# Four 512-column products, then four 256-column ones: the order of TensorE's products in a hybrid mLSTM / RG-LRU / ConvFFN block

## The chip, the cores and the metric

The kernel runs on one core of one Trainium2 chip. The metric is the device time of one execution in microseconds (us). Three runs of the kernel before took 1136.75, 1137.09 and 1137.92 us; the median is 1137.09 us. What this measurement tells from no change is about 0.2% of it, some 2.3 us.

## What is computed

One layer of a streaming encoder over 256 rows of 2048 numbers, all float32:

```python
n1 = rmsnorm(x, norm_mix_g)
q, k, v, o_pre, if_pre, x_r, g_r = split(n1 @ w_in)          # 2048 x (4*1024 + 8 + 2*1024)
h_m = sigmoid(o_pre) * mlstm_chunkwise(q, k, v, i_pre, f_pre)  # 4 heads of 256
h_r = rglru(x_r, ...) * gelu(g_r)                             # 8 blocks of 128
x = x + concat(h_m, h_r) @ w_out                              # 2048 x 2048
gate, up = split(rmsnorm(x, norm_ffn_g) @ w_up)               # 2048 x 2 * 5632
x = x + (silu(causal_dwconv(gate)) * up) @ w_down             # 5632 x 2048
y = rmsnorm(x, norm_final_g)
```

## The kernel before

Nearly all the time is four matrix products with weights that are read once from HBM, 512 KB at a time. TensorE gets them in the type fp32r, and the precision of float32 is kept by splitting each operand in two: a high part (the value rounded to fp32r, written by ScalarE, called ACT in the profile) and a low part (the value minus its high part, written by VectorE, DVE). A product is then high x high + high x low + low x high.

**Projections** (w_in and w_up). The 2048 numbers of a row are 16 k-tiles of 128. `xT[:, kt, 0, :]` holds the high part of k-tile kt of the transposed, normalised input (128 partitions x 256 rows of x), `xT[:, kt, 1, :]` the low part. A **group** is 256 output columns over all 16 k-tiles. Its weights come in four **units** s = 0 to 3 of CH = 4 k-tiles each, in the four slots of a ring: `raw[:, s]` as loaded, `w[:, s, c, 0, :]` the high and `w[:, s, c, 1, :]` the low part of k-tile c of the unit. A group adds up in two banks of PSUM, `ps[:, 2 * pair + n, :]` with n = 0 and 1 for its two halves of 128 outputs; `pair` alternates between groups. In one bank, columns 0 to 255 gather high x high, and columns 256 to 511 the two mixed products. So each k-tile and each n has one product of 512 columns ("full": 128 columns of high weights stand in the array, and the high and low parts of xT stream past) and one of 256 columns ("rest": the low weights stand, the high part of xT streams). For the group of v (`rows_out=True`) the two operands change roles, with the same sizes. Every product has stationary data of its own, 128 x 128, so every product has one load (LDWEIGHTS).

`part_of_unit` writes these products, for a range of k-tiles; `unit` waits until the low weights of a slot are there (`lo_ready`), calls it for four k-tiles and lets the last product signal `unit_used`, which lets ACT write that slot's next weights; `group` waits for the group's banks (`group_free`) and runs four units. There are 24 groups with w_in (q, k of head 0; then v, o, x_r and g_r of each head, and q, k of the next), and 44 with w_up: 68 groups of 64 products, 4352 products in all. In the first group, `after(pe, tiles, ...)` also waits for the low part of each two k-tiles of xT.

**Contractions** (w_out and w_down, function `contraction`, line L1190): here every product is 512 columns wide, and n, the inner loop, alternates between two banks. They aren't touched.

Between groups of a head TensorE also does plain float32 products: scores (L1133, L1135), the weighted values (L1143 to L1146), a row sum (L1151), the RG-LRU gates (L1161). The order on every engine is the order of the code; nothing is scheduled. The lines that the change touches are L1066 (512 columns) and L1068 (256 columns), and for v L1062 and L1064:

Of the kernel before, what the change touches and what calls it, by code (L numbers as in the profile page):

```python
# [33 lines left out]
P = 128  # L34
D = 2048
S = 256
KT = D // P
# [14 lines left out]
CH = 4  # L52
COLS = 256
# [58 lines left out]
def hybrid_block(nc, x, w_in, w_out, w_up, w_down, wa, wx, gate_w, par_in, const_in, gfin_in, out):  # L112
    with ExitStack() as ctx:
# [3 lines left out]
        def sb(name, shape, dt=F32, where=ctx):  # L117
            return where.enter_context(nc.sbuf_tensor(name, shape, dt))
# [4 lines left out]
        xT = sb("xT", [P, KT, 2, S], F32R)  # L123
        raw = sb("raw", [P, RING, HALF])
        w = sb("w", [P, RING, CH, 2, COLS], F32R)
# [64 lines left out]
        ps = ctx.enter_context(nc.psum_tensor("ps", [P, 8, BANK], F32))  # L190
# [56 lines left out]
        def after(eng, steps, name, i=0):  # L247

            eng.wait_ge(steps.sem, steps.after(name, i))
# [783 lines left out]
        def _(pe):  # L1033
            mm = nc.tensor.matmul
# [16 lines left out]

            def part_of_unit(s, pair, tiles_of_k, rows_out=False, tiles=None):

                for c in tiles_of_k:
                    kt = s * CH + c
                    if tiles and c % 2 == 0:
                        after(pe, tiles, f"t{kt // 2}")
                    for n in range(2):
                        full, rest = ps[:, 2 * pair + n, :], ps[:, 2 * pair + n, COLS:2 * COLS]
                        cut = slice(n * P, (n + 1) * P)  # L1060
                        if rows_out:
                            mm(full, xT[:, kt, 0, cut], w[:, s, c, :, :].rearrange("p a n -> p (a n)"),  # L1062
                               start=kt == 0, stop=False)
                            ins = mm(rest, xT[:, kt, 1, cut], w[:, s, c, 0, :], start=False, stop=kt == KT - 1)  # L1064
                        else:
                            mm(full, w[:, s, c, 0, cut], xT[:, kt, :, :].rearrange("p a n -> p (a n)"),  # L1066
                               start=kt == 0, stop=False)
                            ins = mm(rest, w[:, s, c, 1, cut], xT[:, kt, 0, :], start=False, stop=kt == KT - 1)  # L1068
                return ins

            def unit(g, s, pair, rows_out=False, tiles=None):

                pe.wait_ge(lo_ready, g * RING + (s + 1 + RING))
                part_of_unit(s, pair, range(CH), rows_out, tiles).then_inc(unit_used, 1)
# [8 lines left out]
            for n in range(WARM_UP):  # L1083
                ins = mm(ps[:, B_DEN, 0:P], ones[:], ones[:], start=True, stop=True)  # L1084
# [15 lines left out]
            pe.wait_ge(group_free, 1)  # L1100
            pe.wait_ge(first_lo_ready, 1)
            part_of_unit(0, 0, range(CH // 2), tiles=V0)
            transpose_x(1)
            pe.wait_ge(lo_ready, RING + 1)
            part_of_unit(0, 0, range(CH // 2, CH), tiles=V0).then_inc(unit_used, 1)
            transpose_x(2)
            unit(0, 1, 0, tiles=V0)
# [4 lines left out]
            for kt in range(KT):  # L1112
                ins = mm(ps[:, B_SC, :], gws[:, kt, :, :].rearrange("p a n -> p (a n)"),  # L1113
                         xT[:, kt, :, :].rearrange("p a n -> p (a n)"), start=kt == 0, stop=kt == KT - 1)
# [175 lines left out]
```

## Time and profile before

| | |
|---|---|
| median of three runs | 1137.09 us |
| span of the profiled execution | 1135.8 us |
| TensorE products (PE) | busy 1125.2 us, 99% |
| TensorE loads (PEld) | busy 968.0 us, 85% |
| VectorE (DVE), ScalarE (ACT), GpSimd (POOL) | 749.2, 578.7, 51.6 us |
| HBM | 188 GB/s over the span |

A row of TensorE's products shows its start, which is measured, and an end that is modelled and lies behind the start of the next product, since products are pipelined. How long a product holds the engine is therefore read from start to start. "PEclk" is the granted clock of TensorE in tenths of full speed in the page, and as a share of it in the windows view; full speed is 2.4 GHz.

### The profile page before, as it was taken

The page shows a single profiled execution, that of the slowest core. Times are in us where ns is not written, and L with a number is a line of the kernel's source. Part 1 is how long each engine was busy: PE and PEld are TensorE (multiplying, and loading weights), DVE is VectorE, ACT ScalarE, POOL GpSimd, SP SyncE. Part 2 cuts the span into 40 slices and gives each one's busy share as a digit, 9 for nine tenths or more (in the row PEclk, how much of TensorE's full clock was granted, in tenths as well). Part 3 has the DMA queues.
Part 4 walks back from the last instruction along what each step waited for, and adds up shares of the span by engine and source line. Part 5 has one row for each costly group of instructions (what it writes and reads, how often), then busy time and mean ns, then how long its engine had stood idle before and what let it go on. Part 6 is the DMA issues. An engine that isn't in the chain of part 4 may idle for free.

```text
span 1135.8 us, 18132 instructions
## 1 busy us (share of the span) xinstructions
PE 1125.2 (99%) x6030; PEld 968.0 (85%) x6030; DVE 749.2 (66%) x989; ACT 578.7 (51%) x768; POOL 51.6 (5%) x48
## 2 busy tenths in 40 slices
PE   9999999999999999999999999999999999999997
PEld 8888888888888888888888888888888888888886
DVE  6768576595776686666666666766666655556554
ACT  6656464564665664344434444443544545555454
POOL 0100100100000000000000000000000000002000
PEclk9999999999999999999999999999999999999999
DMA  8756657657555466656665665666566565655653
GB/s 265 226 161 186 191 150 205 167 166 194 183 199 196 153 185 206 190 161 215 191 184 173 211 190 165 204 201 186 167 208 195 190 196 190 194 192 186 196 190 114
DMA packets 166617, 213.56 MB, mean 188 GB/s; under 512 B 6940, under 2 KB 149532, under 8 KB 166464
## 3 DMA queue, kind: packets, MB, share of 16 engines
q1 hardware_dynamic: 165456, 210.40, 60.2%
q0 software_dynamic: 560, 2.24, 0.6%
q10 hardware_dynamic: 576, 0.60, 0.2%
q8 instruction: 15, 0.25, 0.1%
q14 instruction: 10, 0.08, 0.0%
HBM read 211.10 MB, written 2.11 MB: 188 GB/s over the span
## 4 chain that ended last, share of the span: by engine, by line
PE 95%; DVE 3%; ACT 1%; issue 0%; DVEq 0%; ACTq 0%
PE ps L1066 41%; PE ps L1190 27%; PE ps L1068 20%; PE ps L1062 3%; PE ps L1064 1%; DVE w L612 1%; PE ps L1161 0%; PE ps L1041 0%; DVE aT L618 0%; ACT w L351 0%; PE ps L1084 0%; PE ps L1113 0%; PE ps L1143 0%; PE ps L1133 0%; DVE xT L663 0%
## 5 line engine op out<-in xcount | busy, mean ns | idle before, releaser
L1066 PE MATMUL ps<-xT,w 128*128 128x512 f32 x2048 | 716.7, 396 | 1.0 <-DVE w L678 0.5
L612 DVE TENSOR_TENSOR w<-raw,w 128x1024 fp32r<-128x1024 f32 x391 | 479.1, 1237 | 342.9 <-ACT w L351 341.9
L351 ACT ACTIVATE w<-raw 128x1024 fp32r<-128x1024 f32 (+1 forms) x393 | 409.7, 1055 | 417.2 <-PE ps L1068 247.6
L1068 PE MATMUL ps<-xT,w 128*128 128x256 f32 x2048 | 569.2, 278 | 0.0
L1066 PEld LDWEIGHTS ps<-xT,w 128*128 128x128 f32 x2048 | 384.2, 188 | 91.1 <-DVE w L612 1.0
L1068 PEld LDWEIGHTS ps<-xT,w 128*128 128x128 f32 x2048 | 385.2, 188 | 0.2
L1190 PE MATMUL ps<-w,aT 128*128 128x512 f32 x1440 | 327.9, 389 | 0.9 <-DVE aT L618 0.9
L1190 PEld LDWEIGHTS ps<-w,aT 128*128 128x128 f32 x1440 | 269.8, 188 | 57.6 <-DVE aT L618 1.7
L351 ACT ACTIVATE fs<-fc 128x512 f32<-128x512 f32 x22 | 13.9, 632 | 101.0 <-DVE fc L962 101.0
L1025 POOL TENSOR_TENSOR fs<-fs,rB 128x512 f32<-128x512 f32 x22 | 28.4, 1293 | 569.5 <-ACT fs L351 569.5
L1062 PE MATMUL ps<-w,xT 128*128 128x512 f32 x128 | 45.2, 398 | 0.0
L618 DVE TENSOR_TENSOR aT<-act,aT 128x256 fp32r<-128x256 f32 x88 | 38.9, 442 | 0.0
L962 DVE SCALAR_TENSOR_TENSOR fc<-fg,par,fc 128x256 f32<-128x256 f32 x88 | 36.6, 477 | 0.0
L1064 PE MATMUL ps<-w,xT 128*128 128x256 f32 x128 | 35.8, 280 | 0.0
L351 ACT ACTIVATE aT<-act 128x256 fp32r (+1 forms) x88 | 35.3, 401 | 0.0
L351 ACT ACT_TABLE_LOAD x23 | 29.5, 1283 | 2.6 <-issue 2.2
L1062 PEld LDWEIGHTS ps<-w,xT 128*128 128x128 f32 x128 | 24.0, 188 | 5.9
L1064 PEld LDWEIGHTS ps<-w,xT 128*128 128x128 f32 x128 | 24.1, 189 | 0.0
L958 DVE TENSOR_SCALAR fc<-fg,par 128x256 f32<-128x256 f32 x44 | 16.2, 410 | 4.1 <-DVE fg L952 4.0
L969 DVE TENSOR_TENSOR act<-fu,fs 128x512 f32 (+1 forms) x22 | 15.2, 693 | 4.9 <-DVE fu L623 4.8
L351 ACT ACTIVATE xn<-xres 128x512 f32<-128x512 f32 (+3 forms) x15 | 13.3, 889 | 8.6 <-DVE xres L898 8.6
L663 DVE SCALAR_TENSOR_TENSOR xT<-ps,par,xT 128x256 fp32r<-128x256 f32 x32 | 13.3, 477 | 6.2 <-ACT xT L351 6.2
(147 smaller groups left out, 391.8 us busy)
## 6 DMA issues: line engine op xcount, KB each, us to landing
raw<-w_up_dram SPq DMA_DIRECT2D x176, 512.0 KB, 4.6
raw<-w_in_dram SPq DMA_DIRECT2D x95, 512.0 KB, 3.9
raw<-w_down_dram SPq DMA_DIRECT2D x88, 512.0 KB, 4.6
raw<-w_out_dram SPq DMA_DIRECT2D x32, 512.0 KB, 4.6
xres<-x_dram SPq DMA_DIRECT2D x3, 512.0 KB, 7.8
y_dram<-xn SPq DMA_DIRECT2D x3, 384.0 KB, 3.1
bc<-rows POOLq DMA_DIRECT2D x4, 256.0 KB, 6.9
gfin<-gfin_dram POOLq DMA_DIRECT2D x1, 1024.0 KB, 4.6
```

Source lines behind the costliest of these rows:

```text
L351: return sc.activation(out_, in_, fn, **kw)
L612: v.tensor_tensor(w[:, s, :, 1, :], raw[:, s, :].rearrange("p (c n) -> p c n", c=CH), w[:, s, :, 0, :], ALU.subtract).then_inc(lo_ready, 1)
L618: v.tensor_tensor(aT[:, s, 1, :], src[:, bass.ds(first + s, 1), :].rearrange("p a n -> p (a n)"), aT[:, s, 0, :], ALU.subtract).then_inc(a ...
L958: did(v.tensor_scalar(fc[:, b, :], tap, fpar(b, k), fpar(b, FTAPS), ALU.mult, ALU.add), V3, f"c{b}_{k}")
L962: did(v.scalar_tensor_tensor(out=fc[:, b, :], in0=tap, scalar=fpar(b, k), in1=fc[:, b, :], op0=ALU.mult, op1=ALU.add), V3, f"c{b}_{k}")
L969: did(v.tensor_tensor(act[:, bass.ds(j * 2, 2), :], fu[:], fs[:], ALU.mult), V3, "act")
L1025: did(nc.gpsimd.tensor_tensor(fs[:], fs[:], rB[:].to_broadcast([P, 2, S]), ALU.mult), L3, "fs_r")
L1062: mm(full, xT[:, kt, 0, cut], w[:, s, c, :, :].rearrange("p a n -> p (a n)"), start=kt == 0, stop=False)
L1064: ins = mm(rest, xT[:, kt, 1, cut], w[:, s, c, 0, :], start=False, stop=kt == KT - 1)
L1066: mm(full, w[:, s, c, 0, cut], xT[:, kt, :, :].rearrange("p a n -> p (a n)"), start=kt == 0, stop=False)
L1068: ins = mm(rest, w[:, s, c, 1, cut], xT[:, kt, 0, :], start=False, stop=kt == KT - 1)
L1190: ins = mm(ps[:, bank0 + 2 * r + n, :], aT[:, s, a_part, cut], w[:, s, 2 * n:2 * n + 2, w_part, :], start=opens and s == 0 and a_part == 0 ...
```

## The change

The four k-tiles of a unit are taken two by two. For each two, the four 512-column products come first (k-tile c0 with n = 0 and 1, then c0 + 1 with n = 0 and 1), then the four 256-column products in the same order. Before, each 512-column product was followed by the 256-column product of the same k-tile and bank.

```diff
-                for c in tiles_of_k:
-                    kt = s * CH + c
-                    if tiles and c % 2 == 0:
-                        after(pe, tiles, f"t{kt // 2}")
-                    for n in range(2):
-                        full, rest = ps[:, 2 * pair + n, :], ps[:, 2 * pair + n, COLS:2 * COLS]
-                        cut = slice(n * P, (n + 1) * P)
-                        if rows_out:
-                            mm(full, xT[:, kt, 0, cut], w[:, s, c, :, :].rearrange("p a n -> p (a n)"),
-                               start=kt == 0, stop=False)
-                            ins = mm(rest, xT[:, kt, 1, cut], w[:, s, c, 0, :], start=False, stop=kt == KT - 1)
-                        else:
-                            mm(full, w[:, s, c, 0, cut], xT[:, kt, :, :].rearrange("p a n -> p (a n)"),
-                               start=kt == 0, stop=False)
-                            ins = mm(rest, w[:, s, c, 1, cut], xT[:, kt, 0, :], start=False, stop=kt == KT - 1)
+                for c0 in tiles_of_k[::2]:
+                    if tiles:
+                        after(pe, tiles, f"t{(s * CH + c0) // 2}")
+                    for low in range(2):
+                        for c in (c0, c0 + 1):
+                            kt = s * CH + c
+                            for n in range(2):
+                                bank = 2 * pair + n
+                                cut = slice(n * P, (n + 1) * P)
+                                if low:
+                                    held, moved = (xT[:, kt, 1, cut], w[:, s, c, 0, :]) if rows_out else (w[:, s, c, 1, cut], xT[:, kt, 0, :])
+                                    ins = mm(ps[:, bank, COLS:2 * COLS], held, moved, start=False, stop=kt == KT - 1)
+                                else:
+                                    held, moved = (xT[:, kt, 0, cut], w[:, s, c, :, :]) if rows_out else (w[:, s, c, 0, cut], xT[:, kt, :, :])
+                                    mm(ps[:, bank, :], held, moved.rearrange("p a n -> p (a n)"), start=kt == 0, stop=False)
```

On TensorE, in the first unit of the program (its first two k-tiles; L1041 are the transposes of x, `dve_step` the wait for xT), a piece of the difference:

```order
 L1099 MATMUL ps<-ones 128x128 x6
-L1066 MATMUL ps<-xT,w 128x512 [waits dve_step,first_lo_ready,group_free]
-L1068 MATMUL ps<-xT,w 128x256
+L1068 MATMUL ps<-xT,w 128x512 [waits dve_step,first_lo_ready,group_free]
+L1068 MATMUL ps<-xT,w 128x512 x3
+L1065 MATMUL ps<-xT,w 128x256 x4
 L1041 MATMUL ps<-cst,xres 128x128 [waits x_landed1]
```

The two rows of before stand four times in turn; the new numbers of the lines are L1068 for 512 columns and L1065 for 256. The first product has the same waits, and no product behind it waits, in either order.

On TensorE, at the start of a group in the loop over w_up (L1073 is the head of `unit`), before:

```order
L1073 ISA [waits group_free]
L1066 MATMUL ps<-xT,w 128x512 [waits lo_ready]
L1068 MATMUL ps<-xT,w 128x256
L1066 MATMUL ps<-xT,w 128x512
L1068 MATMUL ps<-xT,w 128x256
```

and after, up to the next unit:

```order
L1073 ISA [waits group_free]
L1068 MATMUL ps<-xT,w 128x512 [waits lo_ready]
L1068 MATMUL ps<-xT,w 128x512 x3
L1065 MATMUL ps<-xT,w 128x256 x4
L1068 MATMUL ps<-xT,w 128x512 x4
L1065 MATMUL ps<-xT,w 128x256 x4
L1073 REGISTER_ALU
```

A unit has the same sixteen products, and the first has the same wait; eight changes of width in it have become two runs of 4 + 4. The orders of all other engines are the same in both kernels.

## Rows read from the trace of the kernel before

**Rows 1.** The page: busy time, slices of PE and its clock, chain by line.

```profile
span 1135.8 us, 18132 instructions
PE 1125.2 (99%) x6030; PEld 968.0 (85%) x6030; DVE 749.2 (66%) x989; ACT 578.7 (51%) x768; POOL 51.6 (5%) x48
...
PE   9999999999999999999999999999999999999997
...
PEclk9999999999999999999999999999999999999999
...
PE ps L1066 41%; PE ps L1190 27%; PE ps L1068 20%; PE ps L1062 3%; PE ps L1064 1%; DVE w L612 1%; PE ps L1161 0%; PE ps L1041 0%; DVE aT L618 0%; ACT w L351 0%; PE ps L1084 0%; PE ps L1113 0%; PE ps L1143 0%; PE ps L1133 0%; DVE xT L663 0%
```

**Rows 2.** Windows by stage: start, head groups, w_out, w_up, w_down, end.

```profile
core 0: us, PE busy (x) PEld busy (x) DVE busy (x) ACT busy (x) POOL busy (x), PEclk, DMA share, GB/s
0.00:39.00 39.00, 36.53 (x207) 32.14 (x208) 27.71 (x63) 28.63 (x53) 1.46 (x6) 1.00 0.72 224
39.00:320.00 281.00, 280.54 (x1582) 244.14 (x1581) 195.02 (x258) 158.74 (x200) 15.95 (x18) 1.00 0.63 183
320.00:402.00 82.00, 82.00 (x380) 68.37 (x381) 54.97 (x75) 47.03 (x75) 0.00 (x0) 1.00 0.59 193
402.00:888.00 486.00, 486.00 (x2810) 425.17 (x2809) 325.68 (x409) 218.43 (x254) 28.45 (x22) 1.00 0.61 188
888.00:1128.00 240.00, 239.57 (x1059) 198.04 (x1058) 142.79 (x184) 122.89 (x183) 5.76 (x2) 1.00 0.56 184
```

**Rows 3.** Groups of instructions: the page's part 5.

```profile
L1066 PE MATMUL ps<-xT,w 128*128 128x512 f32 x2048 | 716.7, 396 | 1.0 <-DVE w L678 0.5
...
L351 ACT ACTIVATE w<-raw 128x1024 fp32r<-128x1024 f32 (+1 forms) x393 | 409.7, 1055 | 417.2 <-PE ps L1068 247.6
L1068 PE MATMUL ps<-xT,w 128*128 128x256 f32 x2048 | 569.2, 278 | 0.0
L1066 PEld LDWEIGHTS ps<-xT,w 128*128 128x128 f32 x2048 | 384.2, 188 | 91.1 <-DVE w L612 1.0
```

**Rows 4.** Timeline in a group of w_up: start us, length us.

```profile
600.12 0.27 PE L1068 MATMUL ps<-xT,w 128*128 128x256 f32 x1
600.12 0.19 PEld L1066 LDWEIGHTS ps<-xT,w 128*128 128x128 f32 x1
600.23 0.40 PE L1066 MATMUL ps<-xT,w 128*128 128x512 f32 x1
600.23 0.19 PEld L1068 LDWEIGHTS ps<-xT,w 128*128 128x128 f32 x1
600.46 0.28 PE L1068 MATMUL ps<-xT,w 128*128 128x256 f32 x1
600.47 0.19 PEld L1066 LDWEIGHTS ps<-xT,w 128*128 128x128 f32 x1
600.58 0.39 PE L1066 MATMUL ps<-xT,w 128*128 128x512 f32 x1
```

**Rows 5.** Timeline, PE, w_up: two products 64 places apart.

```profile
500.05 0.39 PE L1066 MATMUL ps<-xT,w 128*128 128x512 f32 x1
...
511.14 0.39 PE L1066 MATMUL ps<-xT,w 128*128 128x512 f32 x1
```

**Rows 6.** Timeline, PE, head 0: two products 64 places apart.

```profile
89.19 0.40 PE L1066 MATMUL ps<-xT,w 128*128 128x512 f32 x1
...
100.49 0.40 PE L1066 MATMUL ps<-xT,w 128*128 128x512 f32 x1
```

**Rows 7.** The chain in order of time: start us, length us, what.

```profile
23.92 3.67 PE ps L1113 x16
...
85.50 1.73 PE ps L1161 x8
...
158.75 1.73 PE ps L1161 x8
...
230.76 1.73 PE ps L1161 x8
...
888.48 130.60 PE ps L1190 x576
```

**Rows 8.** Timeline of the scores of head 0, plain float32.

```profile
51.55 0.63 PEld L1135 LDWEIGHTS ps<-qT,kT 128*128 128x128 f32 x4
...
51.76 0.61 PE L1135 MATMUL ps<-qT,kT 128*128 128x128 f32 x4
```

## The prediction, made before the changed kernel was run

> **What bounds the kernel now.** I read the page first. TensorE's products are busy for 1125.2 of 1135.8 us, every slice but the last is at 9, and the chain that ended last runs through the projection lines for two thirds of the span and through L1190 for another 27% [rows 1]. So the kernel is as long as TensorE's row of products, and what one product adds from start to start is the price of everything. The windows by stage say that this holds in each stage apart: TensorE is idle for 2.5 us in the first 39 us, 0.5 us up to 320, and not at all over w_out and over the 486 us of w_up, with its clock granted in full, 1.00, which is 2.4 GHz [rows 2]. In the groups of instructions the 2048 products of L1066 found TensorE idle for 1.0 us in total, and those of L1068 never; ACT, on the other hand, waited 417.2 us in front of its high parts, mostly for L1068, which is the signal at a unit's end [rows 3]. The engines that feed TensorE have time over. The order inside a unit does not move that signal: the last product of a unit is a 256-column one before and after, and it ends when all sixteen are done.
>
> Next, how long one product holds the engine. The lengths in the groups (396 and 278 ns) overlap and are no use for this. In the contraction, where all products are 512 wide, 576 of them take 130.60 us [rows 7]: 226.7 ns from one to the next. I call the 512-column product A and the 256-column one B, so A to A is 226.7 ns. In w_up 64 products, half of each kind, take 511.14 - 500.05 = 11.09 us [rows 5]: an A and a B together hold the engine for 2 x 11.09 / 64 = 346.6 ns. Subtracting, a B costs 119.9 ns. The difference of 106.8 ns between A and B for 256 more columns is 2.4 columns per ns, the full clock; what is left is 13.3 ns in either, 226.7 - 213.3 and 119.9 - 106.7. The time of a product is thus its columns plus a constant, and the constant is the same where widths alternate and where they don't.
>
> The same pair is not always as cheap. In head 0, 64 products take 100.49 - 89.19 = 11.30 us [rows 6], 176.6 ns each in place of 173.3: 3.3 ns more per product. I call this the wide spacing and the other the narrow one. It lasts for stretches. From the gates' products of one head to those of the next (64 x 6 projection products and the same small ones) it is 73.25 us from 85.50, and 72.01 us from 158.75 [rows 7], so six groups at wide spacing cost 1.24 us more than at narrow spacing: 384 x 3.3 ns = 1.27 us, the same. The sixteen 512-column products of L1113 have it too, 3.67 / 16 = 229.4 ns [rows 7]. It begins and ends where plain float32 products stand between groups. The trace doesn't say why.
>
> **The change part by part.** No instruction is added or removed: 4352 products, with as many loads, move inside their units. The unit's wait, its signal and the other engines' orders stay. Half of the products change their neighbour. Before, the engine goes A to B and B to A only, 4 + 4 times in eight products, at 4 x 346.6 = 1386.4 ns. After, eight products hold three A to A, one A to B, three B to B and one B to A. Three of the four kinds are in the rows: 3 x 226.7 + 346.6 = 1026.7 ns. The fourth, B to B, does not occur before in fp32r. There are 4352 / 8 = 544 such runs, so 1632 steps from B to B, and the change is worth 1632 x (B to B - 119.9 ns).
>
> Bounds for B to B. From below: plain float32 products of 128 columns follow each other, each with a load, every (0.61 - 0.275) / 3 = 112 ns [rows 8]; 275 ns is taken as the length of one such row (278 ns in the groups' mean for a row of the like streaming time [rows 3]), 0.61 us is that of four. Such products take 216 ns with 256 columns (1.73 / 8 [rows 7]), so 0.81 ns or two clocks per column, and 128 of them stream for 107 ns, like a B. That gives 1632 x -7.9 ns = -12.9 us. From above: the load. If loads could not overlap a product at all, B to B would be at least a load's row of 188 ns [rows 3], and the sum +111 us. I exclude that end: the load that starts at 600.47 has a row of 190 ns, and the A that it is for starts at 600.58, 110 ns later [rows 4]. So a full load already fits behind a B 2176 times in the kernel before; behind another B the same load has the same 107 ns of streaming to hide in. A smaller loss stays possible, if an A that follows a B starts before it can stream, and the row hides it. As a bound for this I take the wide spacing, +3.3 ns on each of these steps: +5.4 us.
>
> Loads are not saved up either. In rows 4 each load starts within 10 ns of the product in front of the one that it serves, behind the long product as behind the short one. If the long products gave a reserve that short ones used up, loads would start earlier there.
>
> The Trainium skill, page "TensorE: Matmul & The Clock Gate", section "Back-to-back issue gap", gives N / 2.4 + 2.5 ns for a matmul, 109.2 ns for 256 columns. By it B to B would be estimated at 109.2 ns, and the sum would be -17.5 us if the other steps kept their measured times. The rows disagree with it for this type: they give 13.3 ns beside the columns, not 2.5. The same page, section "LDWEIGHTS (loading the stationary operand)", puts a load at columns / 1.2, 106.7 ns for 128, which would just fit behind 256 columns in either order. The rows agree so far, since an A starts 110 ns after the load behind a B.
>
> Which value for B to B? The constant of 13.3 ns appears in A to A and in the mean of A to B and B to A to within 0.1 ns. A cost that belonged to the change of width, or to two products in a row in one bank, would have made these two differ. I take 119.9 ns, so the term is 0. A second effect of the order, successive sums into the same PSUM columns, is 240 ns apart after; the four products of rows 8 do it every 112 ns. It costs nothing.
>
> At the start, TensorE waits for xT and the first weights; the first product's wait is the same, and the 2.5 us of idle time stay. Sum: 1135.8 + 0 us of span. The median of runs lies 1.3 us above this execution's span, so 1137.1 us. From no change 0.2%, 2.3 us, can be told.
>
> **The rivals.**
> 1. *Narrow everywhere.* A to A with alternating banks (L1190) is always narrow; L1113, all in one bank, is wide; the projections before put each A and B into one bank and are now one, now the other. After the change no two products in a row share a bank. If sharing is what lets the wide spacing stand, it goes: two times 1.24 us, and up to 256 products of the four groups before 65 us at 3.3 ns, 0.8 us, together -3.3 us: 1133.8 us. Against it: rows 5 share banks too and are narrow.
> 2. *Wide where it was narrow.* Which spacing holds seems settled at the edges between plain and fp32r products, and the change alters what follows there. If the 44 groups of w_up take the wide one, it is 2816 x 3.3 = +9.3 us: 1146.4 us.
> 3. *Short products starve for loads* (the other side of my forecast). In the run of four B each load must fit behind a B, with no A between to catch up. It decides from 1.4 ns per step, 2.3 us / 1632, so from 121.3 ns. At my bound of +3.3 ns it is 1142.5 us. For it speaks only that A after B may start early; against it the equal constants.
> 4. *Short products run closer.* With B to B at 112 ns, 1124.2 us. For it speaks that one A starts 110 ns after its B, the next 120 [rows 4]; against it that this is made up by the A, which then lasts longer.
>
> **How the numbers follow.** No change 0.50 (1136 to 1139 us), rival 1 0.15, rival 2 0.13, rival 3 0.12, rival 4 0.10. Rivals 1 and 4 are faster by over 0.2%, 0.25; 2 and 3 slower, 0.25; same 0.50. The predicted time is the likeliest case, 1137.1. The range of 8 in 10 takes in rival 1 and the price of rival 2, 1132 to 1147 us; it leaves out most of rival 4 and the far tail of 3.
>
> **What would show it.** In the changed kernel's timeline, four A should start 226.7 ns apart, and the Bs 119.9; sixty-four products in w_up should take 11.09 us, the 486 us of w_up should stay 486, and w_down, which isn't touched, 240. If the total moves, the sixty-four products tell which case: 11.30 us means rival 2, B to B above 121 or near 112 ns with A to A kept means rival 3 or 4; equal lengths from gates to gates in all heads, near 72.0 us, mean rival 1. The forecast is wrong if the constant of 13.3 ns belongs not to a product but to its neighbours.

## The result, and the profile after

The changed kernel takes 1143.44 us (five runs, 1143.10 to 1143.55), the kernel before 1137.84 us in the same session. The ratio is 1.0051, with a 95% interval of 1.0040 to 1.0062: 0.5% slower, 5.6 us, clear of the 0.2% that the measurement can tell from nothing. The likeliest case of the prediction, no change, did not come; its range, 1132 to 1147 us, held the time.

From the page of the changed kernel (busy times, slices, the chain by line) and its windows over the stages of [rows 2]:

```profile
span 1141.3 us, 18132 instructions
...
PE 1130.1 (99%) x6030; PEld 972.9 (85%) x6030; DVE 749.5 (66%) x989; ACT 578.6 (51%) x768; POOL 51.8 (5%) x48
...
PEclk9999999999999999999999999999999999999999
...
PE ps L1068 43%; PE ps L1190 27%; PE ps L1065 22%; DVE w L612 1%; PE ps L1161 0%; DVE aT L618 0%; DMA xres<-x_dram 0%; PE ps L1041 0%; ACT w L351 0%; PE ps L1113 0%; PE ps L1143 0%; PE ps L1133 0%; ACT xn L351 0%; DVE xc L820 0%; DVE xT L663 0%
```

```profile
0.00:39.00 39.00, 35.98 (x207) 31.51 (x208) 27.94 (x63) 28.61 (x53) 1.46 (x6) 1.00 0.72 224
39.00:320.00 281.00, 280.51 (x1583) 245.12 (x1582) 195.18 (x258) 158.97 (x201) 15.92 (x18) 1.00 0.63 183
320.00:402.00 82.00, 82.00 (x383) 68.44 (x382) 54.76 (x76) 46.98 (x75) 0.00 (x0) 1.00 0.59 193
402.00:888.00 486.00, 486.00 (x2775) 424.81 (x2773) 322.08 (x401) 213.64 (x247) 27.32 (x21) 1.00 0.61 188
```

No new wait has come: TensorE is still never idle over w_up, idle for 0.5 us in the heads, and its clock is granted in full. In the first 39 us it is idle for 3.0 us where it was 2.5, but the kernel isn't later for it: the gates of head 0 start at 85.42 us, and at 85.50 before [rows 7]. Yet in the same 486 us of w_up it gets through 2775 products where it did 2810 [rows 2]. The products themselves stand further apart. The chain of the changed kernel in order of time shows where (start, length, what; a length here runs to the next piece's start):

```profile
85.42 1.73 PE ps L1161 x8
...
158.16 1.73 PE ps L1161 x8
...
230.90 1.73 PE ps L1161 x8
...
395.95 2.74 PE ps L1190 x12
...
600.64 0.93 PE ps L1068 x4
601.57 0.47 PE ps L1065 x4
602.04 0.93 PE ps L1068 x4
602.97 0.48 PE ps L1065 x4
...
893.93 130.62 PE ps L1190 x576
```

A run of four A (512 columns) takes 0.93 us, 232.5 ns for each, not the 226.7 of [rows 7]. A run of four B (256 columns) takes 0.47 or 0.48 us, 119 ns each, a shade less than the 119.9 forecast. Over 64 products, from this timeline of the changed kernel,

```profile
502.24 1.09 PE L1068 MATMUL ps<-xT,w 128*128 128x512 f32 x4
...
513.47 1.09 PE L1068 MATMUL ps<-xT,w 128*128 128x512 f32 x4
```

it is 11.23 us: between the 11.09 us of the narrow and the 11.30 us of the wide spacing [rows 5, 6], 2.1 ns per product above narrow. From gates to gates the heads take 72.74 us twice (85.42, 158.16, 230.90), where they took 73.25 and 72.01 [rows 7]. The wide and the narrow stretches have both gone, and nearly one spacing is left (175.4 ns a product, in a few groups of the heads 175.0). The untouched w_down takes 130.62 us for 576 products, as before.

So the balance is: 4352 products x 2.1 ns = +9.1 us against all-narrow, less what the wide stretches had cost the kernel before, two heads of 1.24 us and up to 0.8 us at the start, 3.3 us. That makes +5.8 us; the spans differ by 5.5 us, the medians by 5.6 us. The chains say where it is lost. In the kernel before, the last piece of w_out stands at

```profile
396.27 2.74 PE ps L1190 x12
```

and w_down starts at 888.48 [rows 7]. So the changed kernel comes to w_up 0.32 us sooner (395.95), takes 495.24 us for it in place of 489.47, 5.77 us more, and starts w_down 5.45 us later.

### The profile page after: what moved, and what is told of

Read it like the earlier page. It is cut to its first block, busy times and chain, and to the rows that moved or that the text cites. A ratio compares the mean times of both kernels' runs of the same rounds, so it can differ in the third digit from the quotient of the medians.

```text
span 1141.3 us, 18132 instructions
## 1 busy us (share of the span) xinstructions
PE 1130.1 (99%) x6030; PEld 972.9 (85%) x6030; DVE 749.5 (66%) x989; ACT 578.6 (51%) x768; POOL 51.8 (5%) x48
## 4 chain that ended last, share of the span: by engine, by line
PE 95%; DVE 3%; ACT 1%; issue 0%; DMA 0%; DVEq 0%; SPq 0%; ACTq 0%
PE ps L1068 43%; PE ps L1190 27%; PE ps L1065 22%; DVE w L612 1%; PE ps L1161 0%; DVE aT L618 0%; DMA xres<-x_dram 0%; PE ps L1041 0%; ACT w L351 0%; PE ps L1113 0%; PE ps L1143 0%; PE ps L1133 0%; ACT xn L351 0%; DVE xc L820 0%; DVE xT L663 0%
## 5 line engine op out<-in xcount | busy, mean ns | idle before, releaser
L1068 PE MATMUL ps<-xT,w 128*128 128x512 f32 x2048 | 561.6, 396 | 1.3 <-issue 0.7
L1068 PEld LDWEIGHTS ps<-xT,w 128*128 128x128 f32 x2048 | 350.6, 189 | 49.2 <-DVE w L612 1.1
L1065 PEld LDWEIGHTS ps<-xT,w 128*128 128x128 f32 x2048 | 314.1, 189 | 43.7
L1065 PE MATMUL ps<-xT,w 128*128 128x256 f32 x2048 | 325.7, 281 | 0.0
L1068 PE MATMUL ps<-w,xT 128*128 128x512 f32 x128 | 35.0, 395 | 0.0
L1068 PEld LDWEIGHTS ps<-w,xT 128*128 128x128 f32 x128 | 21.9, 189 | 2.9
L1065 PEld LDWEIGHTS ps<-w,xT 128*128 128x128 f32 x128 | 19.6, 189 | 2.7
L1065 PE MATMUL ps<-w,xT 128*128 128x256 f32 x128 | 20.4, 281 | 0.0
L351 ACT ACTIVATE xn<-xres 128x512 f32<-128x512 f32 (+3 forms) x15 | 13.3, 888 | 8.6 <-DVE xres L898 8.6
L663 DVE SCALAR_TENSOR_TENSOR xT<-ps,par,xT 128x256 fp32r<-128x256 f32 x32 | 13.3, 477 | 5.7 <-ACT xT L351 5.7
```

The costliest lines, as they stand in the source:

```text
L351: return sc.activation(out_, in_, fn, **kw)
L663: ins = v.scalar_tensor_tensor(out=xT[:, kt, 1, :], in0=ps[:, 4 + b % 4, n * S:(n + 1) * S], scalar=par[:, gains + kt:gains + kt + 1], in1 ...
L1065: ins = mm(ps[:, bank, COLS:2 * COLS], held, moved, start=False, stop=kt == KT - 1)
L1068: mm(ps[:, bank, :], held, moved.rearrange("p a n -> p (a n)"), start=kt == 0, stop=False)
```

## The experiments

The extra per product is counted in each trace over 13.3 ns beside the columns, the constant of the narrow spacing. All-narrow would be some 1134.5 us, the kernel before less its 3.3 us. The kernels write the products of a unit as a list `(low, c, n)`, low = 1 for the 256-column ones, and run through it.

**Runs of two**, a k-tile at a time:

```diff
+                products = [item for group_of in cs for item in [(low, group_of, n) for low in range(2) for n in range(2)]]
```

> Per k-tile: two 512-column products, then two 256-column ones. The trace of the changed kernel shows 16 products of w_up in 2807 ns where the kernel before has 2773, and at the start of w_down about ten 512-column products that are dearer than 226.7 ns after the width changed. Theory 'settling': a product costs more for about ten places after a change, the first two 512-column ones about 235 ns each, less what the 256-column ones give back; a run of 2 + 2 then costs 5 to 16 ns more than two pairs, 1140 to 1152 us in all. Rival 'price per change': each pair of changes of width costs the 16.7 ns found for runs of 4, however long the run; twice as many changes cost 4352 / 4 x 16.7 = 18.2 us over all-narrow (1134.6 us): 1153 us. Rival 'banks': only the change of bank at each product matters, then it is as in the changed kernel, 1143.4 us.

1138.69 us, ratio 1.0012 (1.0003 to 1.0021) to 1137.16 us. All three theories were wrong: the price per change of width by a wide margin, settling by at least 1.3 us. The stretch from the end of w_out to w_down, 395.95 + 2.74 to 893.93 or 495.24 us in the changed kernel, is 491.77 us here:

```profile
395.15 2.74 PE ps L1195 x12
...
889.66 130.60 PE ps L1195 x576
```

The kernel before has 489.47 us there, narrow throughout. So the order of two and two costs 2.30 us / 2816 = 0.8 ns per product.

**Runs of eight**, all A of a unit, then all B:

```diff
+                products = [item for group_of in [cs] for item in [(low, c, n) for low in range(2) for c in group_of for n in range(2)]]
```

> Per unit: eight 512-column products, then eight 256-column ones. Settling: the first eight 512-column products of w_down after the change of width cost 1856 ns in the changed kernel, 43 ns more than eight at 226.7; less the 6 ns that four 256-column products give back, about 37 ns per 16 products, 4352 / 16 x 37 = 10 us over all-narrow (1134.6 us): 1144.7 us. Price per change: half as many changes as in the changed kernel, 4.5 us over all-narrow: 1139.2 us. Banks: 1143.4 us.

1140.60 us, ratio 1.0030 (1.0019 to 1.0042): between the two theories again, 1.25 ns per product. The chain shows the run itself:

```profile
600.25 1.84 PE ps L1073 x8
602.09 0.95 PE ps L1070 x8
603.04 1.84 PE ps L1073 x8
```

Eight A take 1.84 us. If the first four take 0.93 us, as in runs of four, the other four take 0.91 us, 227.5 ns each: the dear ones are the first few behind the short products, and then it is the 226.7 ns of the contraction. Eight B take 0.95 us, 119 ns each. My 'settling' estimate, 10 us over all-narrow, was nearly double the 6 us measured, because it took the start of w_down in the changed kernel as the measure of every run of A behind short ones. At that start the dear A reach to the ninth place, inside w_up to the fifth. Windows of 0.05 to 0.1 us in the changed kernel give the starts of the first, fourth, eighth and twelfth product of w_down; on the average the products between them stand 233, 230 and 230 ns apart:

```profile
893.77 0.40 PE L1190 MATMUL ps<-w,aT 128*128 128x512 f32 x1
894.47 0.62 PE L1190 MATMUL ps<-w,aT 128*128 128x512 f32 x2
895.39 0.62 PE L1190 MATMUL ps<-w,aT 128*128 128x512 f32 x2
896.31 0.62 PE L1190 MATMUL ps<-w,aT 128*128 128x512 f32 x2
```

**One bank twice**: runs of four, with n outside and the two k-tiles inside.

```diff
+                products = [item for group_of in cs[::2] for item in [(low, group_of + d, n) for low in range(2) for n in range(2) for d in range(2)]]
```

> Runs of four and four as in the changed kernel, but the two k-tiles are the inner loop and n the outer one: two products in a row go to one bank, and no two products in a row stream the same data. If only the widths in a row set the time (settling and price per change alike), it is as the changed kernel, 1143.4 us, with 2807 ns for 16 products. If the bank matters or the shared stream of n = 0 and 1, it differs by over 2 us.

1143.64 us, ratio 1.0057 (1.0043 to 1.0071), the time of the changed kernel. In runs of four, neither the bank nor the stream shared by two products in a row matters.

**Alternate widths and alternate banks** (units 1 to 3 of a group):

```diff
+                products = [(low, c, (turn + low) % 2) for turn in range(2) for c in cs for low in range(2)] if s else [(low, c, n) for c in cs for n in range(2) for low in range(2)]
```

> The widths alternate one by one as in the kernel before, but in units 1 to 3 of each group each product goes to the other bank than the one ahead of it (first the 512-column products of n = 0 with the 256-column ones of n = 1 over the four k-tiles, then the other way round). If only the widths matter it is as the kernel before, 1137.8 us, with wide and narrow stretches in the heads. If sharing a bank is what lets the wide spacing stand, the heads are narrow and it is 1134.6 to 1135.4 us. If the change of bank costs time, it is near 1143 us.

1137.30 us, ratio 1.0004 (0.9995 to 1.0013). The heads still have both spacings: its gates stand 72.00 and 73.25 us apart,

```profile
86.21 1.73 PE ps L1166 x8
...
158.21 1.73 PE ps L1166 x8
...
231.46 1.73 PE ps L1166 x8
```

now with the narrow one first. So sharing a bank is not what lets the wide spacing stand. Nor did this edit put the narrow one first: the run e6 below leaves the heads' instructions as they were in the kernel before, and its gates stand 72.01 and then 73.25 us apart:

```profile
85.52 1.73 PE ps L1170 x8
157.53 1.73 PE ps L1170 x8
230.78 1.73 PE ps L1170 x8
```

Which head has the wide spacing is thus not fixed by the order of the products.

**All short**: each A cut into two B, with a load of its own for each.

```diff
+                        for a, b in ((0, 0), (0, 1), (1, 0)):
+                            half = slice(0, COLS) if a == b else slice(COLS, 2 * COLS)
+                            ins = mm(ps[:, bank, half], held, moved, start=kt == 0 and a == b, stop=kt == KT - 1 and a == 1)
```

> Each 512-column product of the projections is cut into two of 256 columns (high x high, high x low), so a group has 96 products of 256 columns in a row and its own load for each, 2176 products and loads more in all; the output is the same sum. If a 256-column product behind another holds the engine for 119.9 ns, as the prediction took it, a group takes 96 x 119.9 = 11.51 us in place of 11.09, and the kernel 68 x 0.42 = 28.6 us more than all-narrow, 1163 us. If loads could not keep up in a long run of short products, it would be over 1166 us; if short products run closer in a long run (112 ns), 1111 us or the pace of the other engines.

1163.01 us (four runs), ratio 1.0224 (1.0208 to 1.0239). Timeline:

```profile
599.82 2.44 PE L1067 MATMUL ps<-xT,w 128*128 128x256 f32 x19
```

(2.44 - 0.28) / 18 = 120.0 ns from B to B, load after load. The step that the prediction had to guess was right, and loads keep up with short products.

**One part alone**: four and four in w_up (e6), or in the heads (e7).

```diff
+            runs = [1]    # e7: 4; products in runs of this many, alternating for 1
...
             contraction(G_OUT, OUT_BODIES, 0, G_OUT, E2, transpose_early, transpose_late)
+            runs[0] = 4   # e7: 1
```

> The order of four and four in the 44 groups of w_up alone; the heads keep the alternating order. The traces so far give each product of an order of its own extra over 13.3 ns: alternating 0 (narrow) or 3.3 (wide), runs of two 0.8, of four 2.1, of eight 1.25. If these are additive, w_up loses 2816 x 2.1 = 5.9 us: 1143.0 us. If the loss of the changed kernel sits elsewhere (start, edges), it stays near 1137.2 us.

> The order of four and four in the 24 groups of w_in alone. It costs 1536 x 2.1 = 3.2 us and takes away the wide spacing of some 970 products, 3.2 us: no change against the kernel before, 1137.2 us, and the gates of successive heads are 72.6 to 72.8 us apart in all heads. If the wide stretches had nothing to do with the order, it would be 1140.4 us.

1143.40 us, ratio 1.0053 (1.0039 to 1.0067), and 1137.91 us, ratio 1.0002 (0.9993 to 1.0011). Both are as the additive reading has it, e6 within 0.4 us. w_up loses all of it. In the heads the new order costs what the wide stretches had cost, and all of them are alike:

```profile
85.39 1.73 PE ps L1170 x8
...
158.13 1.73 PE ps L1170 x8
...
230.88 1.73 PE ps L1170 x8
```

**A seed in each unit**: the first k-tile in the order A A B B, the other three alternating.

```diff
+                    products = [(low, ck[0], n) for low in range(2) for n in range(2)]
+                    products += [(low, c, n) for c in ck[1:] for n in range(2) for low in range(2)]
```

> The first k-tile of each unit has two 512-column and then two 256-column products; the other three k-tiles alternate as before. Theory 'the spacing is a cycle that the last few products select': a fixed pattern at each unit's head puts all units into one and the same cycle, whatever stood before. If that is the narrow one, the units' other 12 products have 173.3 ns and the kernel 1134 to 1136 us; if the wide one, 176.7 ns and 1145 to 1149 us. Rival, 'the plain float32 products select it and nothing else does': heads keep stretches of both kinds, w_up stays narrow but for the price of its heads, 0.8 x 4 of 16 products, 1138 us.

1141.35 us, ratio 1.0036 (1.0022 to 1.0049), and neither theory. In its w_up the units go narrow, wide, narrow, wide. Between the two seeds of this timeline, and behind the second, five pairs each:

```profile
600.91 0.39 PE L1074 MATMUL ps<-xT,w 128*128 128x256 f32 x2
601.13 0.40 PE L1077 MATMUL ps<-xT,w 128*128 128x512 f32 x1
...
602.87 0.39 PE L1077 MATMUL ps<-xT,w 128*128 128x512 f32 x1
...
603.68 0.40 PE L1074 MATMUL ps<-xT,w 128*128 128x256 f32 x2
603.91 0.40 PE L1077 MATMUL ps<-xT,w 128*128 128x512 f32 x1
...
605.68 0.40 PE L1077 MATMUL ps<-xT,w 128*128 128x512 f32 x1
```

1.74 us and 1.77 us. No plain float32 product and no wait lies between. The wide spacing is thus a thing that the stream of fp32r products carries on without a wait or a plain float32 product, and four products in another order can start or end it.

**Seeds to steer it** (e9 to e12), each the kernel before with the k-tile order above at a few places:

```diff
                     unit(g0 + 3, s, 1)      # e9, e10, e12: seed for s == 3, behind L1161
                 unit(1, s, 1)               # e10 also: seed for s == 0
             group(G_UP + 1, ...)            # e11 only: written out, seed for s == 0
                     group(g0 + 4, ...)      # e12 also: seed for s == 0
```

> The kernel before, with one k-tile in the order two of 512, two of 256 columns in each head: the first k-tile of the unit behind the plain float32 gate products (L1161 of the kernel before), at which the spacing went over in every head. In the run with such a k-tile at the head of every unit, w_up changed from narrow to wide and back at each unit, so one of them seems to turn the state over. Theory 'a state that is turned over': two turns cancel, the spacing of a head stays as it was when it reached the gates, and with the narrow one of head 0 all heads stay narrow: gates to gates 72.0 us each time, 1134.7 us in all. Rival 'only coincidence of that loop': heads as before, 1137.2 us, or all wide, 1138.5 us.

1139.65 us, ratio 1.0018 (1.0009 to 1.0027). Turned over twice it was not: all heads are wide, 85.62 to 158.86 and to 232.10, 73.24 us each.

> As e9_seed_after_lru, and the same order once more in the first k-tile of group 1 (k of head 0), which runs wide in the kernel before. If one such k-tile turns the state over, group 1 and the groups behind it are narrow, another 0.3 to 0.8 us: 1134.2 us; but then head 0 may reach its gates in the other state than before, and the heads be wide: 1138.5 us. The theory says which from the trace, not ahead: what the scores and the weighted values do to the state differed between runs.

1139.55 us, ratio 1.0017 (1.0008 to 1.0026). In its trace group 1 stays wide, head 0 is narrow up to its gates, and all is wide from the first seed behind them on.

> The kernel before with four products in another order: the second group of w_up is written out ahead of the loop, and its first k-tile has two products of 512 and two of 256 columns; all other 4348 projection products are in the order of before. Theory 'a state that is turned over': from there all of w_up is at the wide spacing, 64 products in 11.30 us, up to the contraction: 43 groups x 64 x 3.33 ns = 9.2 us, 1146.4 us. Rival, 'a change of order costs only where it stands': 1137.2 us.

1137.25 us, ratio 0.9998 (0.9989 to 1.0007). In its trace w_up stays narrow: a seed does not turn every narrow stretch wide. 'A state that is turned over' has fallen.

> As e9_seed_after_lru, and one more k-tile in the order two and two: the first of the group behind (q of the next head; heads 0 to 2). In e9 and e10 the spacing was wide behind each of the first such k-tiles, whichever it was ahead; in e8 such a k-tile inside a wide stretch was followed by a narrow one each time. Theory 'a cycle that the order of the last products selects': each head has 16 wide products and then narrow ones up to the next gates, 72.1 us from gates to gates in every head. Over all-narrow (1137.5 - 3.2 = 1134.3 us) stay the start and perhaps head 0 up to its gates, 0.7 to 1.9 us: 1135.0 to 1136.2 us, less than the kernel before by 1.3 to 2.5 us. Rival, 'the plain float32 products select, and a seed's effect elsewhere was particular to w_up': heads wide as in e9, 1139.6 us.

1137.54 us, ratio 1.0001 (0.9992 to 1.0010). The gates are 72.61 and 72.60 us apart:

```profile
85.62 1.73 PE ps L1172 x8
...
158.23 1.73 PE ps L1172 x8
...
230.83 1.73 PE ps L1172 x8
```

Half of what was expected came: behind the second seed each head is narrow, but the plain products of the scores, which left the spacing alone in the profile of the kernel before, turn it wide again here. Nothing was won, and no version tried is faster than the kernel before by more than the measurement can tell.

## Why the prediction failed where it did

- **What bounds the kernel** held. TensorE without a gap decides, no wait took the place of another, and the time followed the distance of products and nothing else.
- **The step that failed** is "3 x 226.7": A to A was taken from the contraction, where hundreds of A stand in a row. Behind short products the first few A are dearer. These are the mean times in ns from each product's start to the next one's, by place in the run, over all of w_up in each trace:

| order | A, first to last | B, first to last |
|---|---|---|
| alternating (before) | 231.7 | 115.0 |
| runs of two | 233.0, 233.1 | 114.8, 115.9 |
| runs of four (changed kernel) | 234.4, 234.1, 232.5, 228.4 | 117.5, 119.4, 118.8, 118.4 |
| runs of eight | 233.8, 235.5, 228.6, 232.5, 230.8, 226.6, 226.7, 226.7 | 113.3, 118.9, 120.2, then 120.0 |

In the sum of the prediction for eight products, the three A to A took 701.0 ns and not 680.1, the three B to B 355.7 and not 359.7, and A to B with B to A 346.8 where it had 346.6. That is 17.1 ns more, and 544 x 17.1 ns = 9.3 us, the 9.1 us of the balance above.
- **Why it failed.** The sentence "the constant is the same where widths alternate and where they don't" holds for the sum of a pair only. In w_up of the kernel before, an A took 231.7 ns and a B 115.0: the A 5 ns more than the 226.7 put down for it, the B 5 ns less than the 119.9 that was left. So the equal constants could not rule out a price for the change of width: the A pays it and the B behind it gives it back. Rows 4 have it at their grain of 10 ns, 230 from A to B, 110 and 120 from B to A; the prediction saw the 110 under rival 4, called it made up by the A, and did not price an A without a B behind it. The start of w_down in the kernel before says the same: its first seven A stand 230.4 ns apart on the average, and then it is 226.7. And the wide spacing, the same products with the same neighbours at 3.3 ns more on the average, showed that a product's time depends on more than its neighbour. I took two settled patterns for a law of single steps.
- **B to B** was forecast at 119.9 ns. It is 120.0 ns in a long run (e5) and about 119 in runs of four and eight. The number was right, but the way to it was in part luck, since it subtracted an A's time that no A in the alternating stretch had. Neither the bound of 112 ns nor rival 3, short products that starve for loads, came in.
- **Rival 1**, narrow everywhere because no bank is shared, was wrong in its reason (e4, e3). The wide stretches did go, and took 3.3 us off the loss.
- **Rival 2** named the nearest kind of loss, a wider spacing in w_up at 3.3 ns per product, and priced it at 9.3 us. It was 2.1 ns, in w_up and in the heads, a third spacing and not the wide one. The end of the range that held the time is owed to it; that the range held is luck as far as the mechanism goes, since none of the five cases described what came.
- **The size**, then: 2.1 ns x 4352 - 3.3 us = +5.8 us for 5.6 measured, and e6 and e7 show it by parts, 5.6 us in w_up and 0.1 in the heads.
- **What stays open** is the mechanism. Extra per product is 0 for all A in the contractions, all B and the narrow alternation, 0.8 ns for runs of two, 2.1 for four, 1.25 for eight, 3.3 for the wide alternation. The sixteen A of L1113 do not settle at 226.7: in the trace of before their last nine steps are 229 ns on the average (226, 229 and 232 in turn), and nothing here says why. A shared bank and a shared stream are excluded as the cause of the price of runs of four (e3), a shared bank as what holds the wide spacing (e4), and loads that can't keep up with short products as well (e5). That the price sits in the first A behind a run of B is shown by the table: in all four of a run of four, in the first five of eight. Why it is there, and what picks narrow or wide after plain products, is not shown. Each trace is of one execution, so whether other executions of a kernel have the same heads wide isn't known either, and the 3.3 us rests on that one trace. No run changed the loads or the number of instructions ahead, so a cause there was not tested.

The Trainium skill, page "TensorE: Matmul & The Clock Gate", section "Back-to-back issue gap", adds 2.5 ns to the columns' time for a matmul taken by itself; for a stream with a load for each matmul it says that this formula is off. No lasting fp32r stretch here comes near it: 13.3 ns is the least. Plain float32 products are near it: the eight gate products take 1.73 / 8 = 216.2 ns each for 512 clocks (213.3 ns), 2.9 ns more, and from start to start they are 215.6 ns apart, 2.3 ns more.

## What to carry to other kernels

Where TensorE is the bound and never idle, the order of products alone can move the time: by 0.5% here, with the same work, loads and waits. No order tried was faster than strict alternation; runs of two, four and eight pay a few ns on the first long products behind each run of short ones. Longer runs were not tried here. The time of a pair doesn't say how it is shared between the two: read each from its own start to the next start. A time taken from a settled pattern should not be used for single steps of a new one: look for a place in the trace where the pattern begins, and read the first ten products there.

## What the runs showed that was not expected

- fp32r products in strict alternation of 512 and 256 columns have two spacings, 346.6 and 353.1 ns a pair, that last for hundreds of products. They go over at plain float32 products or at four products in another order. The 3.3 ns a product are an average: in the wide stretch from 90 to 122 us of the kernel before, the pairs take 360.9, 349.0 and 350.0 ns in turn, again and again. Which heads get which differs between kernels whose heads have the same instructions in the same order (wide first in before, narrow first in e6 and e11).
- In the contractions, 512-column fp32r products behind a pause or behind other products are dearer for two to eleven places, and then stand 226.7 ns apart. Apart from the first step behind a pause, the steps come within 3 ns from one and the same sequence in all the traces, which a stretch enters early or late: 241, 237, 234, 235, 225, 230, 236, 229, 232, 231, then 227, 226, 227. The second to fifth A in a run of eight take four of its last steps before the 227 (table above). What sets the place of entry is not shown.
- A load of 128 columns for each 256-column product, 6528 of them in a row but for the breaks, costs nothing beyond the 120.0 ns.
